# Latent attention with the keys on the partitions and 512 queries in the row, its sums taken on GpSimd

## The reference, cut to what matters

```python
q = (rms_norm(cq, g_q_a) @ w_q_up).reshape(B, S, 8, 64 + 32)
kv = (rms_norm(ckv, g_kv_a) @ w_kv_up).reshape(B, S, 8, 64 + 64)
k_nope, v_m = kv[..., :64], kv[..., 64:]
qm = jnp.concatenate([q_nope, q_pe], axis=-1)
km = jnp.concatenate([k_nope, broadcast(k_pe)], axis=-1)
# causal attention in blocks of 128 queries, 8 heads, head width 96 for scores and 64 for values
s = einsum('bqhd,bkhd->bhqk', qi, km) * 96 ** -0.5
s = where(kpos <= qpos, s, -inf)
o_mla = einsum('bhqk,bkhd->bqhd', softmax(s, axis=-1), v_m)
...
return x + (concat(o_mla, o_swa) * silu(gate)) @ w_out
```

## Time and profile before

| | before |
|---|---|
| median of 3 runs | 2579.3 us (2576.74 to 2581.92) |
| profiled execution | 2584.97 us, of which span 2583.6 us |
| PE busy in the span | 2400.5 us, 93% |
| DVE, ACT, POOL busy | 1293.3, 572.1, 627.3 us |
| granted clock of TensorE, mean | 0.968 |

### The profile page before, as it was taken

The page is one execution under the profiler, slowest core; times in us unless marked ns, Lnnn a source line. Parts: engine busy times, 40 slices in busy tenths (PEclk is TensorE's granted clock), DMA queues, the critical chain, the costliest instruction groups (busy, mean ns, idle before and its releaser), DMA issues. The chain is left out here.

```text
span 2583.6 us, 26060 instructions
## 1 busy us (share of the span) xinstructions
PE 2400.5 (93%) x9806; PEld 1400.2 (54%) x9806; DVE 1293.3 (50%) x2672; ACT 572.1 (22%) x1310; POOL 627.3 (24%) x528
## 2 busy tenths in 40 slices
PE   8899899989999999999999999999999999599992
PEld 5577556654444444444444666644554644487771
DVE  4344414443467777877645466665501446411115
ACT  3344423321122222222212111111100211011111
POOL 1000000044443454444162000006241043012212
PEclk9999999999999999999999999999999999699996
DMA  4000110112110111011244000003250222558875
GB/s 163 1 1 1 49 66 1 49 63 79 33 33 17 33 33 32 18 33 33 74 123 126 33 5 33 33 1 137 92 195 0 66 81 102 198 161 263 259 225 179
DMA packets 144628, 201.77 MB, mean 78 GB/s; under 512 B 16753, under 2 KB 101617, under 8 KB 144497
## 3 DMA queue, kind: packets, MB, share of 16 engines
q1 hardware_dynamic: 137584, 174.87, 20.5%
q0 software_dynamic: 6912, 25.17, 4.1%
HBM read 162.27 MB, written 37.75 MB: 77 GB/s over the span
## 5 line engine op out<-in xcount | busy, mean ns | idle before, releaser
L170 PE MATMUL banks<-arena 128*128 128x512 f32 (+15 forms) x8158 | 2230.4, 462 | 71.7 <-ACT arena L1050 8.9
L170 PEld LDWEIGHTS banks<-arena 128*128 128x128 f32 (+4 forms) x8158 | 1221.3, 185 | 986.8 <-issue 855.7
L173 PE MATMUL banks<-arena 128*128 128x128 f32 (+2 forms) x1552 | 226.9, 284 | 60.8 <-DVE arena L445 10.3
L173 PEld LDWEIGHTS banks<-arena 128*128 128x128 f32 (+2 forms) x1552 | 183.2, 145 | 132.3 <-issue 80.0
L2081 POOL TENSOR_TENSOR arena<-arena 128x512 f32<-128x512 f32 (+3 forms) x160 | 154.4, 967 | 189.1 <-ACT arena L1895 169.5
L258 POOL TENSOR_TENSOR arena<-arena 128x1 f32<-128x1 f32 (+1 forms) x88 | 56.7, 646 | 521.5 <-DVE arena L2589 323.3
L1367 POOL TENSOR_TENSOR arena<-arena 128x512 f32<-128x512 f32 x15 | 25.3, 1684 | 603.2 <-DVE arena L1102 477.7
L1895 ACT ACTIVATE arena<-arena 128x512 f32<-128x512 f32 (+4 forms) x160 | 81.6, 576 | 325.4 <-DVE arena L1983 324.2
L1954 DVE TENSOR_TENSOR arena<-arena 128x512 f32<-128x512 f32 (+3 forms) x160 | 117.8, 800 | 28.4 <-ACT arena L1887 28.4
L1983 DVE TENSOR_TENSOR arena<-arena,banks 128x512 f32<-128x512 f32 (+4 forms) x160 | 89.7, 628 | 8.2 <-PE banks L173 8.2
L3375 POOL DMA_INDIRECT x_scratch<-arena,places x24 | 37.8, 1577 | 213.4 <-DVE arena L3526 213.4
(11 more groups left out here) (343 smaller groups left out, 1737.0 us busy)
## 6 DMA issues: line engine op xcount, KB each, us to landing
x_scratch<-arena SPq DMA_DIRECT2D x40, 512.0 KB, 2.9
arena<-in_o_w_in_dram SPq DMA_DIRECT2D x32, 512.0 KB, 5.5
arena<-x_scratch SPq DMA_DIRECT2D x32, 512.0 KB, 5.5
arena<-in_w_gate_dram SPq DMA_DIRECT2D x16, 1024.0 KB, 15.2
arena<-in_w_up_dram SPq DMA_DIRECT2D x16, 1024.0 KB, 17.4
arena<-in_w_down_dram SPq DMA_DIRECT2D x16, 1024.0 KB, 8.0
arena<-in_x_dram SPq DMA_DIRECT2D x16, 512.0 KB, 4.5
arena<-in_w_in_dram SPq DMA_DIRECT2D x16, 512.0 KB, 7.2
```

The lines of the kernel that those rows point to most:

```text
L170: return pe.matmul(o, a, b, start=start, stop=stop)
L173: return pe.transpose(o, a, ident)
```

## The change

The 32 steps become 8 units `u` (pair `u // 2`, half `u % 2` of the queries), each with 512 queries in the row and blocks of 128 keys on the partitions: 4 blocks in an even unit, 8 in an odd one. Under the diagonal a block has 512, 384, 256 and 128 queries. Scores of a block and head are made by one product into a ring of four banks (`mla_bank`, `mla_free`), copied into the SBUF by ScalarE, and compared on VectorE with the largest so far. The largest of 128 keys by 512 queries is turned on TensorE (8 per unit), reduced on VectorE, spread over the partitions by TensorE again (8 per unit), and taken off on VectorE in SBUF. Then come the exponential in place, the values' product, and the sum over blocks on GpSimd; TensorE adds up the partitions with a matrix of ones (`pe_mla_sums`), ScalarE copies the sum out, and VectorE takes its reciprocal over 128x512. The gate is made with channels on the partitions, 512 tokens at a time, in two parts around the largest, and needs no turning. SP's two loads wait for the last keys, and the next two for the last sum on GpSimd too. The diff, cut:

```diff
@@ pe_queries
                     P.wait_ge(v_out, NT)
-                    for j in range(4):
-                        pe_mla_first(j)
+                    pe_mla_first()
@@
-        class Pairs:
...
-        def pe_turn(st, i, h):
...
-        def turned_out(st, eng, i, h):
...
-        def pe_pairs(st, scores, values, filler):
...
+        def strips(u):
+            if u % 2:
+                return [(0, 2, 0), (2, 2, 0), (4, 1, 0), (5, 1, 128), (6, 1, 256), (7, 1, 384)]
+            return [(b, 1, 128 * b) for b in range(4)]
...
+        def mla_free(key):
+            P.wait_ge(ml_out_a, mla_place[key] - 3)
+            return mla_bank(key)
...
+            for k in range(4 * part, 4 * part + 4):
+                m = mm(bank(7), w_g1[:, k, 128 * p:128 * p + 128], HT[:, k, 512 * n:512 * n + 512], k == 0, k == 7)
...
+        def pe_mla_sums(u):
+            db = mla_free(("d", u))
+            P.wait_ge(ones_made, 1)
+            for h in range(2):
+                P.wait_ge(ml_sum, 2 * u + h + 1)
+                m = mm(db[64 * h:64 * h + 64, :], ONEM, SUM[h], True, True)
+            m.then_inc(ml_made.sem, 1)
+        def pe_mla_first():
+            for n in range(2):
+                pe_mla_keys(0, n)
+            pe_mla_gate(0, 0)
+        def pe_mla():
+            meet(P, queries_over)
+            for u in range(MLA):
+                pe_mla_scores(u)
+                if u:
+                    pe_mla_gate(u, 0)
+                pe_mla_turn_largest(u)
+                if u:
+                    pe_mla_values(u - 1)
+                    pe_mla_sums(u - 1)
+                pe_mla_spread(u)
+                pe_mla_gate(u, 1)
+                if u in (0, 2, 4):
+                    for n in range(2):
+                        pe_mla_keys(u // 2 + 1, n)
+            pe_mla_values(7)
+            pe_mla_sums(7)
...
+        def act_mla():
...
+                        act.activation(strip(SM[g][h], g, b, lo)[:, 0, :], mla_bank(("s", u, b, h))[:, lo:512],
+                                       ACT.Copy).then_inc(ml_out_a.sem, 1)
+                if u:
+                    act_mla_sums(u - 1)
...
+                        act.activation(w, w, ACT.Exp).then_inc(ml_exp.sem, 1)
+                act_mla_gate(u)
...
+        def dve_mla_out(u):
...
+            vs(vec.reciprocal(DC, DC))
...
+            vs(vec.tensor_tensor(o, o, DC, MUL))
...
+            vec.tensor_tensor(o, o, bank(6), MUL).then_inc(ml_gated.sem, 1)
+        def dve_mla():
...
+            for u in range(MLA):
+                dve_mla_largest(u)
+                if u:
+                    dve_mla_gate(u - 1)
...
+                    vec.tensor_reduce(MXM[:, 4 * h:4 * h + 4], tiled(bank(4 + h), 4), AXX, MAX,
+                                      negate=True).then_inc(ml_known.sem, 1)
...
+                        vec.tensor_tensor(w, w, tiled(bank(4 + h)[:, lo:512], 1).to_broadcast([128, n, 512 - lo]),
+                                          ADD).then_inc(ml_moved.sem, 1)
+                if u:
+                    dve_mla_out(u - 1)
...
+        def pool_mla():
...
+                            m = pool.tensor_tensor(su, strip(SM[g][h], g, 0, 0)[:, 0, :] if g and c == 1 else su, s, ADD)
@@ sp_window
             Y.wait_ge(f_pe, swa_f)
+            mla_made(Y, ("k", 3, 1))
...
-            Y.wait_ge(pv_done, mla.pv + 8)
+            Y.wait_ge(ml_pv, 8)
+            Y.wait_ge(ml_sum, 16)
@@ pool_program
             pool_entry()
+            pool_mla()
```

More of the change, by code:

```diff
@@ L591, in program @@
         f_pe, f_a, gate_done = event("filler_projected"), event("filler_out"), event("gate_ready")
-        class Pairs:
[L596 to L626, removed]
-                k = self.turn[key]
-                if k % 2:
-                    P.wait_ge(pt_a, self.a + k // 2)
-                else:
-                    P.wait_ge(pt_v, self.v + k // 2)
-                return bank(4 + k % 2)
-            def turned(self, eng, key):
-                eng.wait_ge(p_turned, self.t + self.turn[key] + 1)
@@ L737, in program @@
-        OG = [stats(128) for _ in range(2)]
         GE = [XB[2][:, 0:256], XB[2][:, 256:512]]
@@ new lines, in pe_mla_values @@
+        def pe_mla_values(u):
+            p, g = u // 2, u % 2
+            last = 4 * g + 3
+            P.wait_ge(ml_exp, strips_before(u + 1))
+            P.wait_ge(ml_gated, u)
+            for b in range(last + 1):
+                lo = 128 * max(0, b - 4 * g)
+                for h in range(2):
+                    m = mm(bank(6)[64 * h:64 * h + 64, lo:512], VM[:, b, 64 * (2 * p + h):64 * (2 * p + h) + 64],
+                           strip(SM[g][h], g, b, lo)[:, 0, :], b == 0, b == last)
+            m.then_inc(ml_pv.sem, 1)
@@ L862, in act_mla, with act_mla_gate @@
+        def act_mla_gate(u):
+            p, n = u // 2, u % 2
+            C.wait_ge(f_pe, u + 1)
+            C.wait_ge(gate_done, u - 1)
+            act.activation(GXM[n], bank(7), ACT.Tanh, scale=0.5)
+            act.activation(OT[:, p, 512 * n:512 * n + 512], bank(7), ACT.Copy).then_inc(f_a.sem, 1)
         def act_mla():
             meet(C, queries_over)
-            for u in range(10):
-                act_mla_unit(0, u)
-            act_pairs(mla, act_mla_exponentials, act_mla_filler)
@@ new lines, in act_mla, with dve_mla_largest @@
+            act_mla_sums(7)
+        def dve_mla_largest(u):
+            g, at = u % 2, [0, 0]
+            for b in range(4 * g + 4):
+                lo = 128 * max(0, b - 4 * g)
+                for h in range(2):
+                    mla_emptied(V, ("s", u, b, h))
+                    s, mr = strip(SM[g][h], g, b, lo)[:, 0, :], MRM[h][:, lo:512]
+                    if b == 0:
+                        if g == 0:
+                            vs(vec.tensor_copy(mr, s))
+                            at[h] = vs.n
+                        continue
+                    if at[h]:
+                        vec.wait_ge(vs.sem, at[h])
+                    m = vec.tensor_tensor(mr, strip(SM[g][h], g, 0, 0)[:, 0, :] if g and b == 1 else mr, s, MAX)
+                    if b < 4 * g + 3:
+                        vs(m)
+                        at[h] = vs.n
+                    else:
+                        m.then_inc(ml_max.sem, 1)
```

324 lines of the change are left out of this document (143 added, 181 removed).

## The result

The changed kernel takes 2593.59 us (2588.72 to 2596.34, six runs), beside 2579.59 us for the kernel before on the same chip: ratio 1.0051, 95% interval 1.0040 to 1.0062. Measured again later, word for word: 2591.12 us, ratio 1.0040 (1.0027 to 1.0053). It is slower by some 0.45%. The forecast was slower by 5.4 us, with a band of 1 to 11; it came to 14.0, outside that band, and the second time to 0.40%, some 10 us, inside it.

A forecast was written before the change was run, and what follows sets the result against it. TensorE was taken to bound the kernel, but the chain through four engines to set the new time: 128.9 + 99.9 + 83.1 + 25.0 = 336.9, plus 7 for the clock, 343.9, 5.4 us longer: 2585 us, range 2569 to 2600.

The forecast's parts named there:

- The 23 us less on TensorE: TensorE's work from 111.3 us falls from 204 to 181 us, and the saving goes into waits of its own.
- Passages of 25.4 and 27.7: Between starts of taking off: 25.4 us from a short unit to a long one, 27.7 from long to short.
- the sum without the clock: Start, passages and end along the chain put the stage's end at 336.9 us, against 338.5 before.
- the 7 us for the clock: Falls of TensorE's clock at start, passages and end: five, 8.5 us at most, 7 taken, bounds 0 and 20.
- VectorE's chain of 19.7 us: Long to short: taking off, reciprocal and products 12.7 us, copies 1.2, six comparisons 5.8, together 19.7.
- The collision: Long to short: VectorE's six comparisons wait for GpSimd's additions, 5.8 us taken against 2.09 when GpSimd rests.
- VectorE isn't held up: Rival, 14%: comparisons come when GpSimd's sums are done, 3 x 3.7 us less, 2574 us, faster.
- The rival with nine falls: By the skill's rule nine waits (start, seven passages, end) end in a fall, costing 15 us: 2593 us.
- in every unit: Rival, 15%: the clock falls in every unit, also the TensorE-bound long preparation; twelve falls, 20 us instead of 7: 2598.
- the clock holds: Rival, 18%: half gates fill TensorE's gaps enough, so the clock stays up: 336.9, 2578 us, no change.
- GpSimd is now on the path, 25.0 us: Stage's end: GpSimd's last sums, ones, copy, reciprocal and products take 25.0 us from the last taking off.
- Waits of 3 to 5 us before the turnings of even units: Sign in the profile after: TensorE's turnings of the largest wait 3 to 5 us in even units, none in odd.

The follow-up runs named there:

- the run where the clock stayed up at the start: The changed kernel with TensorE summing the weights strip by strip with the ones matrix, in place of GpSimd's additions: 2610.44 us, ratio 1.0122.
- the second profile: The changed kernel profiled once more, word for word, with nothing changed: 2591.12 us, ratio 1.0040.
- with the product freed: The changed kernel with the last unit's values' product in a free bank of the ring instead of bank 6: 2588.68 us, ratio 1.0034.

## Why the prediction was right, and where it was off

**Direction and bound: right, the direction with some luck.** The 23 us less on TensorE did go into its waits. Passages of 25.4 and 27.7 were forecast, and 25.7 and 27.9 measured; their sum was short by 2.3 us of 185, 1.7 of it in the four short-to-long ones. But the sum without the clock was 1.6 shorter than before: "slower" hung on the 7 us for the clock, and most of these were charged where nothing was lost. VectorE's chain of 19.7 us is exact in sum, which is luck, for in its parts two errors cancel: comparisons 4.79, not 5.8, and the copies ahead of them 2.11, not 1.2; I had taken copies as free of GpSimd, and they aren't.

**The collision: right, and shown twice.** Without the sums the passage is 2.5 shorter; without the reciprocal the comparisons stretch to 7.17 and eat most of it. The rival "VectorE isn't held up" falls. Its price, 3.7 a passage, would have been too high as well: 2.5 is all, because TensorE is next.

**The clock, the step that was mis-sized.** I counted five falls of 1.7 us, 7 in all. The profile has six stretches at half clock, together 47.8 us, and three of them cost: 5.7 at the start (one stretch of 13.7 us, over the products and turnings on the chain), 2.5 in the last values' product, 1.8 in the next stage: 10.0 us. In the run where the clock stayed up at the start, the first taking off came at 129.3, so 5.3 of the 5.7 are the clock's; in the second profile the start lost some 4. Those in the three long-to-short passages cost nothing, where I had charged 1.7 each: they lasted 6.8, 3.4 and 6.8 us, and the passages took 27.9 all three times. So the number of falls was about right, their length (one price of 1.7 for each) and their places were not.

The rival with nine falls gave 2593, and 2593.6 and 2591.1 were measured. It is near for another reason than counted: the granted clock fell in none of the four short-to-long passages, the falls of the other three cost nothing, and the whole price is at the two ends. The rule of the Trainium skill that the prediction weighed ("TensorE: Matmul & The Clock Gate", section "HAM oscillation — how this bites in real kernels") has every burst of matmuls behind a wait begin at the lower clock again. The trace agrees for the changed kernel's waits of 2.99 us and more, and not for those of 2.19, 1.02 and 0.56. The rival "in every unit", 2598, falls, and so does "the clock holds".

**The end: half right.** "GpSimd is now on the path, 25.0 us": with the clock up it would have been so (333.06 + 5.6 = 338.7, level with GpSimd's 338.93), and with the product freed it is (26.3, POOL last). That 26.3 is 1.3 over the forecast even so: behind the products with ones the copy, the reciprocal and the two products take 6.1 us to the next stage, not the 4.8 of the sum, for they don't overlap. In the changed kernel the values' product set the end. The step that failed is that I gave the values' product no time of its own and let it begin with the exponentials: it waits for L837 of the unit before, 4.4 us behind them, in a bank that the order of VectorE's work holds.

**Signs named.** Waits of 3 to 5 us before the turnings of even units: not so, 0.56, 2.19 and 1.02; the wait of 3.0 is before the scores, where ScalarE's copies return. Odd units' turnings without a wait, comparisons of about 5, table load in ScalarE's wait: as said. The stage's mean clock is 0.93 from 134 us on, at the bound that I had given, and 0.91 from 111.3 us, where the stage begins: below it. That sign of being wrong came true, and it is the mis-sized step, the low clock of the start above all.

```profile
111.30:348.65 237.35, 205.01 (x761) 100.67 (x761) 156.35 (x223) 110.07 (x220) 83.08 (x88) 0.91 0.07 22
```

## What to carry to other kernels

Taking work off the bounding engine is worth nothing until the chain through the others has been added up; in the passages that sum was good to 1.2% here. A wait of TensorE can cost twice when the clock falls behind it and the work that follows is on the path: fill it with work that is ready (here half a half gate in each of two waits), and look where the filler is missing afterwards. Ask of every late product not only whether its operands are ready, but who still holds its bank.

## What the runs showed that I had not expected

- Score products over 96 rows kept TensorE busy for 12.48 of 12.6 us, and the clock stayed at 0.50 all that time. With 128 rows it was back after 6.8 us. One pair of profiles; open.
- The same wait of 3.44 us in the same program was followed by a fall in seven profiles and by none in one. All 36 waits of 3.0 us (three in each of the twelve profiles) had a fall, within 2 us of their end on either side; the three of 1.96 had one, of six around 2.2 two had, and the shorter ones had none.
- VectorE's copies within SBUF take 0.43 us alone and 1.05 beside GpSimd; L834, a product of two SBUF operands, 0.69 and 1.07. L837, which reads a bank, 0.69 in both.
- VectorE's saving of 3.34 us beside a busy GpSimd was worth 1.3: the later instructions met more of it.
